# An S5 scan split into eight sets that pass through TensorE, VectorE and TensorE one behind the other

## What is computed

```python
def _diag_scan(a, bu, h0):
    bu = bu.at[:, 0].add(a * h0)
    _, h = lax.associative_scan(_lin_combine, (jnp.broadcast_to(a, bu.shape), bu), axis=1)
    return h

def _s5(pc, p, h0):
    ...
    lam_bar = jnp.exp(lam * dt)
    h_f = _diag_scan(lam_bar[0], jnp.einsum('blgc,gpc->blgp', uc, b_bar[0]), h0[:, 0])
    h_b = jnp.flip(_diag_scan(lam_bar[1], jnp.flip(jnp.einsum('blgc,gpc->blgp', uc, b_bar[1]), axis=1),
                              h0[:, 1]), axis=1)
    y = (jnp.real(jnp.einsum('blgp,gcp->blgc', h_f, c_mat[0]))
         + jnp.real(jnp.einsum('blgp,gcp->blgc', h_b, c_mat[1]))
         + p['ssm_d'].astype(f32).reshape(SSM_G, SSM_CH) * u)
    y = jax.nn.gelu(y.reshape(b_, l_, D_C)).astype(pc.dtype)
    out = y * jax.nn.sigmoid(y @ p['w_glu'] + p['b_glu'])
    h_last = jnp.stack([h_f[:, -1], h_b[:, 0]], axis=1)
    return out, h_last
```

## Time and profile before

| | us |
|---|---|
| median of 3 runs (1441.34 to 1446.01) | 1442.24 |
| profiled execution | 1441.92 |
| its span, first to last instruction | 1440.2 |
| scan stage in it, 347.2 to 441.7 | 94.5 |
| PE busy in the span | 1315.2 (91%) |
| DVE busy in the span | 564.0 (39%) |

### The profile page before, as it was taken

One profiled execution on the slowest core, in us unless ns is written; L12 is line 12 of the kernel. 1 busy time (PEld: TensorE's weight loads), 2 busy tenths in 40 slices (PEclk: granted clock), 3 DMA queues, 4 the chain that ended last, 5 costly groups with the idle time before them and its releaser, 6 DMA issues. The chain is left out here.

```text
span 1440.2 us, 26978 instructions
## 1 busy us (share of the span) xinstructions
PE 1315.2 (91%) x8994; PEld 751.4 (52%) x8994; DVE 564.0 (39%) x1701; ACT 339.5 (24%) x675; POOL 322.9 (22%) x388
## 2 busy tenths in 40 slices
PE   4998999898778959999999999999999999999766
PEld 2543644766654534455555555555555555555422
DVE  1282457286331434433333333333333333333158
ACT  4121010165112221122222222222222222222111
POOL 4021140130001000023333332323323333233101
PEclk9899799978589988999999999999999999999978
DMA  9865533553016150282498498989999898683195
GB/s 352 242 155 183 181 136 144 164 159 116 27 59 268 76 232 16 91 332 74 164 394 354 179 396 336 415 341 400 393 383 417 344 417 332 264 337 127 40 423 233
DMA packets 90153, 349.10 MB, mean 242 GB/s; under 512 B 22661, under 2 KB 27924, under 8 KB 62592
## 3 DMA queue, kind: packets, MB, share of 16 engines
q1 hardware_dynamic: 68208, 300.31, 54.2%
q0 software_dynamic: 21040, 46.67, 8.8%
q10 hardware_dynamic: 864, 1.57, 0.3%
HBM read 484.32 MB, written 46.87 MB: 369 GB/s over the span
## 5 line engine op out<-in xcount | busy, mean ns | idle before, releaser
L1906 PE MATMUL banks<-rings,hT 128*64 128x256 f32 x3712 | 420.0, 379 | 1.9 <-ACT hT L1796 1.2
L1906 PEld LDWEIGHTS banks<-rings,hT 128*64 128x64 f32 x3712 | 261.4, 137 | 189.4 <-issue 67.9
L1930 PE MATMUL banks<-downs,hT 128*64 128x512 f32 x928 | 222.0, 600 | 0.9 <-issue 0.9
L1769 POOL DMA_INDIRECT h<-h2D,toks x117 | 118.2, 1011 | 453.9 <-DVE kept L1833 433.7
L1796 ACT ACTIVATE hT<-banks 128x512 f32<-128x512 f32 x116 | 69.3, 597 | 377.7 <-PE banks L1893 377.7
L1782 POOL DMA_INDIRECT yD<-hT,dest x116 | 118.0, 1018 | 131.5 <-ACT hT L1810 129.0
L1866 DVE COPY hT<-banks 128x128 f32<-128x128 f32 x116 | 33.8, 292 | 254.9 <-PE banks L1917 254.9
L1810 ACT ACTIVATE hT<-banks,gain 128x512 f32<-128x512 f32 x116 | 79.7, 687 | 179.3 <-PE banks L1930 179.3
L1930 PEld LDWEIGHTS banks<-downs,hT 128*64 128x64 f32 x928 | 56.1, 138 | 68.4 <-issue 68.4
L1823 DVE COPY info<-wparts 128x20 bf16 x118 | 21.3, 181 | 153.7 <-issue 152.6
L1893 PE MATMUL banks<-ident,h 128*128 128x128 f32 x464 | 76.1, 287 | 0.0
(11 more groups left out here) (452 smaller groups left out, 1512.3 us busy)
## 6 DMA issues: line engine op xcount, KB each, us to landing
rings<-w_e_gate SPq DMA_DIRECT2D x116, 1024.0 KB
rings<-w_e_up SPq DMA_DIRECT2D x116, 1024.0 KB
downs<-w_e_down SPq DMA_DIRECT2D x116, 1024.0 KB
rings<-w_ada SPq DMA_DIRECT2D x12, 2048.0 KB, 11.8
rings<-yD SPq DMA_DIRECT2D x8, 2048.0 KB, 17.2
rings<-w_in SPq DMA_DIRECT2D x4, 2048.0 KB, 12.6
rings<-matD SPq DMA_DIRECT2D x3, 2048.0 KB, 14.9
matD<-rings SPq DMA_DIRECT2D x2, 2048.0 KB
```

Of the source, the lines that this page charges most:

```text
L1769: pool.indirect_dma_start(out=xg[u], out_offset=None, in_=k.h2D, bounds_check=2 * TOK - 1, oob_is_err=False, in_offset=bass.IndirectOffset ...
L1906: last = pe.matmul(bank[par][h * SB:(h + 1) * SB, 0:F], lhsT=lhsT, rhs=w[:, (h * KD + kk) * F:(h * KD + kk + 1) * F], start=(kk == 0), sto ...
L1930: last = pe.matmul(bank[4 + par][h * SB:(h + 1) * SB, :], lhsT=hidT[par][:, kk, :], rhs=down[:, kk * D + h * 512:kk * D + (h + 1) * 512], ...
```

## The change

Each direction is cut in four sets of four groups, eight sets in all, and a set goes through all of it by itself: inputs on PE, turning, scan over 328 columns and two products on DVE, outputs on PE. PE's order is written out by hand so that the inputs of a later set stand between the outputs of earlier ones. vin, turned and H have two buffers of one set each; cH and sH have one for each direction. Of the zeros only the boundary columns are written, for Uf, Ub and decay. The flipped turns come first, on banks 6 and 7. Two of the four parts of the turning back, and of its copies, stand before the last output set; the gate's z runs over the first 128 channels of y before it waits for the second. Semaphores change with it: Y_ready and Y_taken take the place of yb_ready, yb_taken, y_ready, y_taken.

The diff, cut to its core; lines of before that it takes away stand in the functions above and are left out where they moved as a whole:

```diff
-    vin, turned2 = sb("vin", [P, G, SL]), [sb(f"turned{i}", [P, 4, SL]) for i in range(2)]
-    H, cH, sH = sb("H", [P, G, SL]), sb("cH", [P, G, SL]), sb("sH", [P, G, SL])
+    vin, turned, H = ([sb(f"{n}{i}", [P, 4, SL]) for i in range(2)] for n in ("vin", "turned", "H"))
+    cH, sH = ([sb(f"{n}{i}", [P, G, SL]) for i in range(2)] for n in ("cH", "sH"))
...
-        pool.memset(Uf[:, :, :], 0.0)
-        pool.memset(Ub[:, :, :], 0.0).then_inc(u_zero, 1)
+        for z in (Uf, Ub):
+            pool.memset(z[:, :, 0:1], 0.0)
+            last = pool.memset(z[:, :, CL + 1:CL + 2], 0.0)
+        last.then_inc(u_zero, 1)
...
-    halves = [(z, g0, min(GB, G - g0)) for z in range(2) for g0 in range(0, G, GB)]
+    halves = [(z, g0, min(GB, G - g0)) for z in (1, 0) for g0 in range(0, G, GB)]
...
+        for m in range(NM):
+            n = m % 4
+            act.wait_ge(Y_ready, m + 1)
+            if m < 4:
+                act.activation(yb[0:NR, n * 512:(n + 1) * 512], bank[4 + m % 2][0:NR, :], ACT.Copy).then_inc(Y_taken, 1)
+            else:
...
+            if m == 6:
+                turned_back(0)
+                turned_back(1)
+        turned_back(2)
+        turned_back(3)
...
-        v(dve.memset(decay[:, :, :], 0.0))
+        dve.memset(decay[:, :, 0:1], 0.0)
+        v(dve.memset(decay[:, :, CL + 1:CL + 2], 0.0))
...
+        for m in range(NM):
+            i, n, gd, b = m // 4, m % 4, groups(m), 2 * (m % 2)
+            dve.wait_ge(V_ready, m + 1)
...
+            out, other, h = vin[m % 2], turned[m % 2], H[m % 2]
+            tt(out[:, :, :], V, cosT[:, gd, :], ALU.mult)
+            tt(other[:, :, :], W, sinT[:, gd, :], ALU.mult).then_inc(V_taken, 1)
...
+            dve.tensor_tensor_scan(h[:, :, :].rearrange("p g i -> p (g i)"),
...
+            tt(cH[i][:, 4 * n:4 * n + 4, :], h[:, :, :], cosT[:, gd, :], ALU.mult)
+            tt(sH[i][:, 4 * n:4 * n + 4, :], h[:, :, :], sinT[:, gd, :], ALU.mult).then_inc(cs_ready, 1)
+            if m == 5:
+                end_states(0)
+        end_states(1)
...
+        def inputs(m):
...
+            pe.wait_ge(u_taken, 3 * i + (4 * n + 3) // GB + 1)
+            if m >= 2:
+                pe.wait_ge(V_taken, m - 1)
...
+        def outputs(m):
...
+            pe.wait_ge(cs_ready, m + 1)
...
+        for n in range(3):
+            channels(n)
+        pe.wait_ge(mats_in, 48)
+        inputs(0)
+        inputs(1)
+        for n in range(3, 6):
+            channels(n)
+        pe.wait_ge(u_taken, 6)
+        inputs(2)
+        outputs(0)
+        inputs(3)
+        outputs(1)
+        inputs(4)
+        outputs(2)
+        inputs(5)
+        outputs(3)
+        end_states(0)
+        inputs(6)
+        pe.wait_ge(near_in, 16 * Q)
+        outputs(4)
+        inputs(7)
+        outputs(5)
+        outputs(6)
...
+        turn_back(0)
+        turn_back(1)
+        outputs(7)
+        end_states(1)
+        pe.wait_ge(Y_taken, NM)
+        turn_back(2)
+        turn_back(3)
+        pe.wait_ge(glu_in, 32)
         for o in range(2):
+            for i in range(2):
+                pe.wait_ge(yT_taken, 2 * i + 2)
+                for j, (lo, n) in enumerate(((0, LAT), (LAT, CTX))):
```

More of the change, by code:

```diff
@@ L1134, in _, with end_states @@
         dve.wait_ge(rot_in, 32)
[L1135 to L1157 removed]
+        def end_states(i):
+            d = DIRS[i]
             dve.wait_ge(fin_t, i + 1)
@@ L1168, in _, with channels @@
     def _(pe):
-        for n, (z, g0, m) in enumerate(halves):
+        def channels(n):
+            z, g0, m = halves[n]
             if n >= 2:
@@ new lines, in inputs @@
+            pe.wait_ge(u_taken, 3 * i + (4 * n + 3) // GB + 1)
+            if m >= 2:
+                pe.wait_ge(V_taken, m - 1)
+            for g in range(4):
+                gd, u = d * G + 4 * n + g, src[:, 4 * n + g, :]
+                col = slice(g * SL, (g + 1) * SL)
+                pe.matmul(bank[b][:, col], lhsT=XT[:, gd * P:(gd + 1) * P], rhs=u, start=True, stop=True)
+                pe.matmul(bank[b + 1][0:NS, col], lhsT=XT[:, gd * P + NS:(gd + 1) * P], rhs=u, start=True, stop=True)
+                last = pe.matmul(bank[b + 1][NS:P, col], lhsT=XT[:, gd * P:gd * P + NS], rhs=u, start=True, stop=True)
@@ new lines, in inputs @@
+            last.then_inc(V_ready, 1)
+        def outputs(m):
+            i, n = m // 4, m % 4
+            d, out = DIRS[i], bank[4 + m % 2]
+            if m >= 2:
+                pe.wait_ge(Y_taken, m - 1)
+            if i:
+                pe.wait_ge(Y_taken, n + 1)
+                pe.matmul(out[0:NR, :], lhsT=k.flip[0:NR, 0:NR], rhs=yb[0:NR, n * 512:(n + 1) * 512],
+                          start=True, stop=False)
+                for g in range(4):
+                    gg = 4 * n + g
+                    pe.matmul(out[0:NR, g * P:(g + 1) * P], lhsT=Uf[:, gg, 1:SL], rhs=near[:, gg, :], start=False, stop=False)
+            pe.wait_ge(cs_ready, m + 1)
+            for g in range(4):
+                gg = 4 * n + g
+                gd, o = d * G + gg, out[0:NR, g * P:(g + 1) * P]
+                w = slice(gd * P, (gd + 1) * P)
+                pe.matmul(o, lhsT=cH[i][:, gg, 0:NR], rhs=Wc[:, w], start=(i == 0), stop=False)
+                last = pe.matmul(o, lhsT=sH[i][:, gg, 0:NR], rhs=Ws[:, w], start=False, stop=(i == 0 or g == 3))
+            last.then_inc(Y_ready, 1)
@@ L1224, in _, with turn_back @@
-        pe.wait_ge(y_taken, 4)
-        for n in range(4):
+        def turn_back(n):
             h, t4 = n // 2, 4 * (n % 2)
```

125 lines of the change are left out of this document (38 added, 87 removed).

## The result

The changed kernel takes **1410.99 us** (median, 1407.80 to 1414.61) against 1441.99 beside it: a ratio of **0.978, 95% interval 0.9763 to 0.9798**. The forecast was 1406.0 with a range of 1401 to 1420. The profiled execution is the lowest one: 1407.80 us, span 1406.0. Its scan stage goes from 344.13 (SP's first transfer) to 404.11 (DVE's last product), 59.98 us; before it was 347.16 to 441.61, 94.45 by the same marks. That is 34.5 us off (35.9 forecast). What lies ahead of the stage is 3.0 us shorter in this execution and what lies behind it 3.4 us longer; neither holds an edit.

A forecast was written before the change was run, and what follows sets the result against it. PE bounds the scan stage when it has work, DVE in two holes, a chain at the end. Holes 16.2, low clock 7.2 and 5.2, front 4.4, tail 4.0, less 1.3, rounded: 35.9 us off 1441.92, so 1406.0; range 1401 to 1420.

The forecast's parts named there:

- What bounds the stage: Scan stage: PE bounds it when it has work, DVE in two holes (16.2 us together), a chain at the end.
- The front: Start of the scan stage: smaller memsets and flipped turns first let inputs begin sooner, 4.4 us off.
- The wait that appears: DVE's first multiplication: waits some 2.7 us for the DMA of sinT, at no cost, with 1.2 us to spare.
- Sizes of the sets: Scan stage: a DVE set takes 3.89 us, PE's pair of inputs and outputs 4.43 us backward, 6.17 forward.
- rival D: Scan stage: 20 switches between input and output sets cost up to 0.28 us each, 5.6 in all; 1412 us, chance 0.06.
- The second pair of cH and sH is what lets PE go on: Scan stage: with it, outputs of one direction no longer hold DVE back at yb_ready; no separate size given.
- The tail: From the last output to the stage's end: 8.95 us where it was 12.9, 4.0 us off.
- The clock: Scan stage: granted clock 1.00 in all stretches; low clock removed, 7.2 us in backward inputs and 5.2 at output starts.
- rival B: Front of the stage: the clock falls and slows three input sets, turns and outputs(0), plus 7.4 us; 1413 us, chance 0.18.
- C: Scan stage: the clock stays low until the forward outputs, 20.6 us more; 1427 us, chance 0.04.
- E: Scan stage: low clock throughout because alternating sets never raise it, 6 us later than before; 1448 us, chance 0.03.
- F: Scan stage: PE still stops for each set's products, so 16.2 us of holes stay in small pieces; 1422 us, chance 0.03.

The follow-up runs named there:

- the spare scans: Changed kernel with a second scan of the same 328 columns, its result not read, in each of DVE's eight sets: 1411.67 us.
- the first profile: Profiled execution of the changed kernel's first timing, nothing altered: 1407.80 us, stage 59.98 us; median of that timing 1410.99 us.
- dummies: Changed kernel with dummy matmuls into a spare bank, first five at attend's end and one before inputs(2): 1407.53 us; other versions also had more dummies or an early table load.
- packed work ahead of the stage: Changed kernel, scan stage unaltered, with forty dummy matmuls of 128x128 packed at attend's end: 1417.80 us.
- the second profile: Profiled execution of the unaltered changed kernel timed again: 1412.07 us, stage 66.30 us; median of that timing 1409.23 us.
- the dummy told of above: One 128x512 dummy matmul before inputs(2), in the changed kernel with five dummies at attend's end and an early sigmoid table load: 1410.65 us.

## Why the prediction was right, and where it was not

- **What bounds the stage: right.** The holes and PE's own work were read correctly from the earlier trace rows; with one scan for a direction they come back, and the spare scans show that DVE is no longer the bound: each made a set 0.74 us longer, more than the 0.56 by which it was short of PE's pair, and the stage did not grow.
- **The front: right.** Inputs(0) began 3.6 us into the stage (347.78) as forecast, inputs(2) at 11.4 (355.54), as forecast. The wait behind the plain turns was 0.59 us, inside its bounds.
- **The wait that appears: right.** V of set 0 was done at some 350.4 and DVE began at 353.20; it waited some 2.7 us for sinT, as forecast. It cost nothing: PE reached outputs(0) at 358.2, products of set 0 were there at 357.2.
- **Sizes of the sets: right.** DVE 3.88 us (3.89 forecast), scan 0.84 (0.82); PE's pairs 4.44 (4.43) and, from 377.71 to 383.85, 6.14 (6.17). Switches between input and output sets cost nothing (39.46 us busy of 39.50), so rival D falls; its 0.28 us for a switch stood on no row. The rule of the Trainium skill on short tiles ("VectorE: DVE Perf Modes", "The TRN2 errata") agrees in sign with the trace: four scans of 0.84 make 3.36 us where one took 2.89; PE covered it. (The prediction's own row for 328 columns reads PSUM; the product out of SBUF took 0.50 us too.)
- **"The second pair of cH and sH is what lets PE go on": wrong.** One pair gives the same time. The claim took the change's own account of itself; DVE's slack against PE's pair, in the same paragraph, would have told that a wait of DVE there has cover.
- **The tail: right.** From the last output (394.9) 9.2 us, 8.95 forecast; undoing it cost 4.2 us of trace, 4.0 forecast, both with the gate's first half mostly at the low clock.
- **The clock: the step that failed.** The forecast had it at 1.00 all through, at 0.66, and rival B at 0.18. Both happen with the same kernel. Of the twelve profiled executions whose front is that of the changed kernel (with or without dummies), eight show a fall 1.8 to 3.5 us into the stage, three one at 11.2 to 14.2 us, and one none. B's price was about right: 66.30 us with 20.5 us of low clock, against 58.3 without (59.98 less the 1.7 us by which outputs(0), 3.44 us from 358.23 to 361.67, were longer than 1.74) is 8.0, where 7.4 was forecast, or 0.39 us for each us at 0.50. And the measured median lies between the two, 5 us above the forecast and 2 below B. The term of the sum that failed is the low clock, put at nothing from the front on: it measured 1.7 us in one profile and 8.0 in the other. That the time came out inside the range is owed to the range reaching to B; the weight given to B was too small.
- **Why its weight was too small.** The argument against B was a row of transposes alone at 1.00, 146.8 to 150.2. That row stops too soon. The transposes ended at 151.0, and the clock fell at 153.63, 2.6 us behind them, and then stood at 0.50 with PE busy without a break (table of stretches of the kernel before, below the list). So this place does not speak against B. The kernel's own fall in the middle of the flips was put down to the 1.98 us of standing still behind the memset; the falls after the change come at the same place, in the flips, without that wait. By Part 4 of "TensorE: Matmul & The Clock Gate" of the Trainium skill, transposes don't count as busy, and the plain turns would be the cause: the falls at 11 to 14 us, behind the turns and the wait, agree with it, and so does the one at 153.63; those at 1.8 to 3.5 us do not, since they come before the first plain turn. (The flips are plain matmuls with a flip matrix.)
- **Rivals C, E and F** did not occur: with the sets in place the clock was back 1.5 us behind outputs(0) at the latest, and PE showed no wait for DVE's products.

The stretches of the kernel before, behind the transposes of the earlier trace rows:

```profile
151.00:153.60 2.60, 1.82 (x17) 1.68 (x16) 0.75 (x2) 0.00 (x0) 0.00 (x0) 1.00 0.51 203
153.60:168.60 15.00, 15.00 (x82) 13.98 (x81) 0.00 (x0) 0.00 (x0) 0.00 (x0) 0.50 0.68 246
```

**What stays open** is why the clock falls in the stage's first microseconds in some executions and not in others. Shortening PE's stand-still at the boundary from 1.03 to 0.63 us, and filling the wait before inputs(2) and attend's last long wait, did not prevent it; a boundary without any stand-still was not tried, and packed work ahead of the stage did not narrow the times. What the fall costs and where it ends are shown; what sets it off is not.

## What to carry to other kernels

Where one engine stops for another once for each batch, cut the other's work into sets and compare what a set takes on each engine: if it takes longer on the first, the wait is gone, and a mixed order or second buffers may bring little beyond that. Before a forecast puts a stretch at full clock, look at more than one profile of it, since the same kernel can run it at either level; and a stand-still just ahead of a fall is not yet its cause, as taking it away showed here.

## What the runs showed of the hardware

- In the second profile PE was busy with input sets for 8.90 of 8.90 us from 351.0 and the clock stayed at 0.50; where it had not fallen, in the first profile, the same sets ran at 1.00. In the profiles with an early fall it came back in the output sets, with the sets in place in outputs(0) or up to 1.5 us behind it, and once ahead of it, behind the dummy told of above.
- A product out of PSUM and one within SBUF take the same 0.49 to 0.50 us for 328 columns, and an add over 64 partitions takes as long as a product over 128.
- A second scan of the same 328 columns right behind the first makes a set 0.74 us longer, and eight of them, 5.6 us of DVE's time, left the stage's length as it was, to a hundredth of a us.
